# Taking the dummy products of ones out of a transformer pair of blocks on one core

## What is computed

```python
def hybrid_mixer(hn, ...):                   # block 1, mixer
    proj = hn @ w_in                         # 9 parts
    y_ret = silu(rg) * groupnorm(retention(rotary(rq), rotary(rk), rv)) @ w_ret_out   # 4 heads
    y_sb = stick_breaking(sq, sk, sv) @ w_sb_out                                      # 16 heads of 64
    return (sigmoid(ga) * y_ret + sigmoid(gb) * y_sb) @ w_out

h = h + rmsnorm(hybrid_mixer(rmsnorm(h)))    # block 1
h = h + rmsnorm(swiglu(rmsnorm(h)))
h = concat(meta_2, h[:, 16:])                # block 2
h = h + rmsnorm(mixer(rms_norm(h)))          # gated convs: 3 taps and 31 taps + layer norm
h = h + rmsnorm(swiglu_2(rms_norm(h)))
```

## Time and profile before

| | |
|---|---|
| median of 3 runs | 2059.4 us (2056.85 to 2059.65) |
| profiled execution, its own time | 2060.28 us |
| its span | 2058.5 us |
| PE busy | 1997.3 us, 97% |
| DVE, ACT busy | 1095.7 us, 710.2 us |
| mean granted TensorE clock | 0.976 of full |

### The profile page before, as it was taken

The page is one execution under the profiler, slowest core; times in us unless marked ns, Lnnn a source line. Parts: engine busy times, 40 slices in busy tenths (PEclk is TensorE's granted clock), DMA queues, the critical chain, the costliest instruction groups (busy, mean ns, idle before and its releaser), DMA issues.

```text
span 2058.5 us, 25213 instructions
## 1 busy us (share of the span) xinstructions
PE 1997.3 (97%) x10194; PEld 1671.5 (81%) x10194; DVE 1095.7 (53%) x1346; ACT 710.2 (35%) x845; POOL 14.6 (1%) x10
## 2 busy tenths in 40 slices
PE   7999999989999999999999999999999999999996
PEld 6878888878989888898768888887898768888885
DVE  3444646454364554636554454454699664545445
ACT  5554646533232232333332222223423442222222
POOL 0000000000000000000000000000000000000000
PEclk9888989989999999999999999999999999999998
DMA  4001101012212222212312232222122112232231
GB/s 166 23 23 39 62 20 61 21 55 99 87 68 82 71 82 92 81 63 80 124 64 82 102 102 82 102 102 82 61 83 82 42 61 94 90 102 102 82 103 41
DMA packets 23474, 157.53 MB, mean 77 GB/s; under 512 B 2672, under 2 KB 3056, under 8 KB 5360
## 3 DMA queue, kind: packets, MB, share of 16 engines
q1 hardware_dynamic: 23408, 156.59, 22.1%
HBM read 154.48 MB, written 2.10 MB: 76 GB/s over the span
## 4 chain that ended last, share of the span: by engine, by line
PE 85%; DVE 8%; ACT 4%; issue 2%; DMA 1%; DVEq 0%; SPq 0%; ACTq 0%
PE psum L464 27%; PE psum L465 26%; PE psum L466 26%; PE psum L596 2%; PE psum L518 2%; DVE z L1291 2%; DVE normed L1291 1%; DVE h L1320 1%; PE psum L584 1%; ACT w_hi L856 1%; DVE w_lo L1284 1%; ACT std L856 1%; DMA w_raw<-in_units 0%; PE psum L617 0%; ACT X_hi L856 0%
## 5 line engine op out<-in xcount | busy, mean ns | idle before, releaser
L464 PE MATMUL psum<-X_hi,w_hi 128*128 128x512 f32 (+1 forms) x1632 | 603.4, 370 | 5.9 <-DVE X_lo L1300 5.0
L465 PE MATMUL psum<-X_lo,w_hi 128*128 128x512 f32 (+1 forms) x1632 | 596.3, 365 | 0.0
L466 PE MATMUL psum<-X_hi,w_lo 128*128 128x512 f32 (+1 forms) x1632 | 595.5, 365 | 0.0
L856 ACT ACTIVATE w_hi<-w_raw 128x2048 fp32r<-128x2048 f32 x140 | 267.4, 1910 | 411.8 <-PE psum L466 395.3
L1284 DVE TENSOR_TENSOR w_lo<-w_raw,w_hi 128x2048 fp32r<-128x2048 f32 x138 | 315.9, 2290 | 144.4 <-ACT w_hi L856 144.4
L464 PEld LDWEIGHTS psum<-X_hi,w_hi 128*128 128x128 f32 x1632 | 307.7, 189 | 64.2 <-issue 6.7
L465 PEld LDWEIGHTS psum<-X_lo,w_hi 128*128 128x128 f32 x1632 | 307.6, 189 | 49.2 <-issue 2.2
L466 PEld LDWEIGHTS psum<-X_hi,w_lo 128*128 128x128 f32 x1632 | 307.2, 188 | 49.4
L1429 DVE TENSOR_TENSOR acc<-acc,psum 128x512 f32<-128x512 f32 x216 | 142.0, 684 | 86.7 <-PE psum L466 86.7
L464 PE MATMUL psum<-M_hi,w_hi 128*128 128x512 f32 x352 | 136.9, 389 | 0.0
L465 PE MATMUL psum<-M_lo,w_hi 128*128 128x512 f32 x352 | 136.9, 389 | 0.0
(11 more groups left out here) (237 smaller groups left out, 2658.4 us busy)
## 6 DMA issues: line engine op xcount, KB each, us to landing
w_raw<-in_units SPq DMA_DIRECT2D x140, 1024.0 KB, 4.8
h<-in_xfm SPq DMA_DIRECT2D x4, 528.0 KB, 5.4
h<-in_xfm SPq DMA_DIRECT2D x1, 2112.0 KB, 7.5
decay<-in_dec SPq DMA_DIRECT2D x4, 512.0 KB, 4.7
out<-h SPq DMA_DIRECT2D x4, 512.0 KB, 2.8
rot<-in_consts SPq DMA_DIRECT2D x1, 528.0 KB, 11.6
acc<-in_consts SPq DMA_DIRECT2D x1, 448.0 KB, 9.0
vec<-in_vecs SPq DMA_DIRECT2D x1, 108.0 KB, 3.7
```

The source lines that it names most:

```text
L464: nc.tensor.matmul(dst, w2[0], x2[0], start=first, stop=False, skip_group_check=True)
L465: nc.tensor.matmul(dst, w2[0], x2[1], start=False, stop=False, skip_group_check=True)
L466: m = nc.tensor.matmul(dst, w2[1], x2[0], start=False, stop=last, skip_group_check=True)
L856: return nc.scalar.activation(out_, in_, f, **kw)
```

## The change

All eleven calls of `keep_warm`, and the function, are taken out. Where a call was the only thing in an `else`, the branch goes too. Nothing else is touched: no wait, no buffer, no order of what stays. The dummy products are not moved, and on the other engines no instruction is changed. Line numbers behind the function become smaller (`logs` is line 589 instead of 596).

```diff
@@ -519,15 +519,8 @@
-        def keep_warm(n, bank=5):
-
-
-            for _ in range(n):
-                nc.tensor.matmul(psum[:, bank, 0:P], ones[:, :], ones[:, :], start=True, stop=True)
-
         pe.wait_ge(ones_ready, 1)
         sums(0, FULL)
-        keep_warm(36)
@@ -661,8 +654,6 @@
                 unit(at, dj, ds, "D", SEQ, y, range(4))
-            else:
-                keep_warm(24, 2)
             logs(g + 2)
@@ -673,7 +664,6 @@
             else:
                 pe.wait_ge(strip_free, at.strip(11) + 1)
-                keep_warm(20, 2)
             logs(g + 3)
@@ -787,9 +777,7 @@
         out_product("w_out", from_x, 1, counted(m_split_lo, 0))
-        keep_warm(16)
         sums(2, SEQ)
-        keep_warm(14)
@@ -828,7 +814,6 @@
             unit(at, j, 4 * j, "R", SEQ, y2, None, counted(y2_ready, 0) if j == 0 else None)
-        keep_warm(45)
         for t in range(CT):
@@ -837,15 +822,12 @@
-        keep_warm(30, 4)
         at = Place("w_out2_b").four()
...
         sums(5, SEQ)
-        keep_warm(16)
         sums(6, SEQ)
-        keep_warm(14)
         ffn("_2", 1)
```

## The result

The changed kernel takes 2070.79 us (median of 5 runs, 2066.46 to 2072.35), the kernel before 2059.4 us (5 runs, 2056.62 to 2060.54). The ratio is 1.0054, with a 95% interval of 1.004 to 1.0069: slower by 0.5%, where 2070 had been forecast. The profiled execution of the changed kernel took 2070.94 us. One of the kernel before's 54 executions in this document took 6892.62 us and enters no ratio.

The account below looks back on a forecast made before the run. PE was taken to bound the kernel, dummies being worth only the clock they keep for work behind them. Terms 6.0 + 0 + 3.3 + 1.4 + 0 + 0 = +10.7 us gave a 2070 us median, range 2065 to 2077 (chance 0.73).

Parts of the forecast that it names:

- Taking them out frees nothing at the borders: At the norm borders PE has no other work ready in the dummies' place, so removing them saves no time.
- First product after a border: Next stage's first unit at three borders: meets a low clock without slack, +2.0 us each, +6.0 together (4.8 to 7.2).
- Sums after the first gap: Border sums run late at a low clock, then catch up: 0 us, at most 2.8 a border.
- Conv stage: Low clock after idle time: mean products +1.7, variance +0.9, first products of w_out2_b +0.7; together +3.3 us (1.7 to 7.6).
- The variance's +0.9: Conv stage's four variance products: nearer to full clock since the mean products can bring it back; 0 to +3.5 us.
- Last quad: End of attention: `logs` start earlier (-0.5 us) but may run at low clock (+1.9); together +1.4 (-0.5 to +1.9).
- First quad 0, start 0: First quad's gain or loss hidden by the sp_all_lo wait (-1.1 to +1.3 us); start's low clock fits waits (0 to +2.6).
- the clock holding at the borders: Rival: clock stays at 1.00 at the borders, only the last quad changes; 2059 to 2063 us, chance 0.10.
- Falls that last long: Rival: clock low through all sums, variance products and 6.7 us of each first unit; +23 us, 2083, chance 0.07.
- Half the throttled time lost: Rival: every low us costs half, eleven places with 56 us low, 28 us lost; 2088 us, chance 0.05.
- The rival of the attention stage: Attention gains 5.9 us by avoiding the fall from 113.7 us, other falls cost under 1.8; 2054 us, chance 0.05.
- the sign that I had named: Prediction counts as wrong if the attention stage moves by more than 3 us either way.

Follow-up runs that it names:

- borders_back: The changed kernel with the 16 and 14 dummies put back at the three norm borders only; 2060.61 us, ratio 1.0022 to the kernel before.
- attention_back: The changed kernel with the 36, 24 and 20 dummies of start and attention stage put back only; 2064.84 us, ratio 1.0045 to the kernel before.
- half_counts: The kernel before with half the dummies at the borders and in the conv stage, all the earlier ones kept; 2067.22 us, ratio 1.0039.

## Why the prediction was right

Direction, size and mechanism held. That the sum, 10.7 us, is exactly the measured distance of the two profiled executions is luck: 6.0 for the borders, 3.3 for the conv stage and 1.4 for the attention stage had been forecast, and 4.9, 6.4 and -0.6 measured. The conv stage's 3.1 us too little made up for 1.1 and 2.0 too much. Over more executions the terms do better: the ratios above give 5.7, 3.6 and 0.9 us, each to some 2.7 us.

- *Taking them out frees nothing at the borders.* Right: the first product starts with the distance that was there ahead of the border (-0.68 us at the first; +8.4 both at `std` and at the first product of the third).
- *First product after a border, 2.0 us each (1.6 to 2.4), 6.0 together.* Somewhat high: 1.2, 1.5 and 2.2, together 4.9. The low stretch that meets them is 3.4 to 6.8 us long, and of that not all lies behind the first product. Over the five kernels without (or with half) the dummies there, 15 borders, the steps go from 1.2 to 2.7 us, mean 1.7.
- *Sums after the first gap, 0.* Right, and in the way forecast: they are late, then caught up.
- *Conv stage, +3.3 (1.7 to 7.6).* Undersized for this execution: 6.4. The mean's +1.7 measured 1.8, and 0.3 came ahead of it. The variance's +0.9 measured 2.6, and w_out2_b's +0.7 measured 1.7. I had reasoned that the mean products bring the clock back; in this execution the fall lasted 17 us, through all of mean and variance. In borders_back and attention_back, which lack the same dummies, the variance cost 0.0 and 1.4 us, and the conv stage 3.1 and 4.2 in all: the term is spread from nothing to 2.6, and +0.9 was within it.
- *Last quad, +1.4.* The mechanism is right: in the changed kernel's chain the logs take twice as long and `a_f` waits for them, against the earlier trace rows:

```profile
427.06 5.36 PE psum L589 x20
432.42 0.02 issue
432.44 1.37 ACT a_f L838 x3
```

  Its sp_lo starts at 425.35, 1.6 us ahead of the earlier trace rows, and its logs end 0.4 us behind (432.42 for 429.27 + 2.74 = 432.01), so the place lost 2.0 us. Where the distance is taken there (from 425 to 434 us), the four executions without the 20 dummies lose 1.2 to 2.0 us, two with them 0.2. But at 455 us, behind the stage, both groups stand the same 1.0 to 1.3 us further back than at 425, so that this loss reaches the end is not shown.
- *First quad 0, start 0.* At their own places they are right: with a low stretch from 20.4 to 27.2 us the distance of the changed kernel is the same at 15 and at 45 us, as in the three others that lack the dummies there, and from 103 to 134 us these four move by -1.0 to +0.1 us. The stage as a whole can't be told from what it does by itself. At its end the four executions with the changed kernel's attention code stand at -6.3, -5.3, -0.6 and +0.9 us, the three with all its dummies at -2.6, -2.3 and 0. In the four 92 to 102 us up to the end of the last quad are at 0.50, in the three 82 to 85: the dummies there do keep the clock, but what that buys is lost in the spread. The expectation that attention_back would match the changed kernel holds as far as that spread lets one see. My bounds for the three terms together went from -1.6 to +5.8 us; two of the four executions lie outside, at -6.3 and -5.3, and by the sign that I had named (the stage moves by more than 3 us) these two would have spoken against the prediction. A spread of 7 us belonged in the range.

Of the rivals, the clock holding at the borders is out: it fell at all of them. Falls that last long came true in the conv stage alone, with 17 and 10 us; at the borders the six low stretches are 3.4 or 6.8 us long. Half the throttled time lost: by the mean clocks the changed kernel has 2 x (1 - 0.959) x 2069.2 = 170 us at the low clock, the kernel before 2 x (1 - 0.976) x 2058.5 = 99. Half of the 71 more is 36 us, and 10.7 were lost. That rule of the Trainium skill (TensorE: Matmul & The Clock Gate, Terms) is an upper bound here, since PE has slack in most of that time. The rival of the attention stage needed two things. A gain of more than 4.1 us there was found in two of the four executions, more often than I had thought; but the borders and the conv stage cost 11.3 us in the changed kernel where it asked for less than 1.8, so it is out.

## What to carry to other kernels

Work without a result can be worth its place where PE would be idle for some 2 us or more ahead of dense products; price it by the work behind the gap that somebody waits for, at 0.47 us for each us it would run low, and nothing where PE has slack. It has to fill nearly the whole gap (half of the dummies saved next to nothing at the borders) and should use the whole array (a quarter of its rows held the clock at three of six gaps of the borders and not in the conv stage), and it must end before the data come. When such a kernel is tuned already, look for the waits that were left out: filling four of them, with two shortened, took 12 us off the median here (9 of them placed in the trace), as much as the eleven places together are worth.

## What was not expected of the hardware

- A busy PE does not keep the clock by itself: with 32 of 128 rows, 17.00 us of 17.00 busy ran at 0.50. Yet the same dummies, in runs of 3.4 to 3.8 us at the borders, have no fall behind them at three of six gaps.
- The same instructions take 7 us more or less in the attention stage from one execution to the next, and their low stretches fall on other places. The runs of the kernel before go from 2050.07 us, with a mean clock of 0.981, to 2060.59 us, with 0.976. That the attention stage makes this difference is likely, not shown: only one execution of this kernel has its stages on record.
- A fall needs no long gap: 2.15 us of idle time at a border of half_counts had one behind it. The waits of 1.53 to 1.66 us that stand ahead of the borders had none where the gap behind them was filled, and sums with many short pauses, 6.04 us of work in 10.10, ran at 1.00 in the changed kernel.
